# Two transformer blocks on one core: stationary and streamed tiles at other distances modulo 512 bytes

## The chip, the cores and the metric

The kernel runs on one core of a Trainium2 chip. The metric is the device time of one execution in microseconds, the median of several runs. Engines are named as in the profile: PE is TensorE's matmul, PEld its weight load, DVE is VectorE, ACT is ScalarE, POOL is GpSimd, and SPq is the DMA queue of SyncE.

## The reference

The input is one sequence of 256 rows of 2048 float32 values. Two unlike transformer blocks follow each other, and everything is float32. Cut to its matrix products, which are all that bears on the change:

```python
h = rms_norm(x, norm_mix_w);  proj = h @ w_in            # 2048 x 6160
x = x + concat(band_attention, gated_linear_attention) @ w_out      # 2048 x 2048
h = rms_norm(x, norm_ffn_w);  u = conv(h @ w_ffn_up)     # 2048 x 11264
x = x + (gelu(u_gate) * u_val) @ w_ffn_down              # 5632 x 2048
x = x + sigmoid(rms_norm(x) @ w_ple_gate) * (p @ w_ple_proj)
h = rmsnorm(rms_norm(x)); proj = h @ w_in_2              # 2048 x 8704
x = x + (sigmoid(ga) * (ya @ w_branch_a) + sigmoid(gb) * (yb @ w_branch_b)) @ w_out_2
x = x + swiglu(rmsnorm(x), w_ffn_in_2, w_ffn_down_2);  out = rmsnorm(x)
```

## The kernel before, in words

**Three matmuls for one product.** A float32 operand is split into a high part, rounded to the type F32R, and a low part, the rest. A product is then hi x hi + hi x lo + lo x hi, each with operands of type F32R. The activations are split once per stage into a pair of stationary tiles. The names of these pairs are AH/AL, BH/BL, XH/XL, ZH/ZL, MH/ML and the small PTH/PTL. The weights are split chunk by chunk as they arrive.

**The stream.** A chunk is two k-tiles of 128 rows by 512 columns, 512 KB. SP loads it into one of four slots of WR (L332), ACT copies WR to WH (L900), DVE subtracts to get WL (L1253), and PE runs `chunk` (L456 to L466): for both k-tiles and both row blocks of 128 it multiplies three times, 12 matmuls per chunk. There are 892 chunks (C_END, L71). Each matmul loads a block of 128 x 128 float32 of the stationary tile (512 bytes of each partition) and streams 512 columns of WH or WL (2048 bytes of each partition) past it into a bank of `acc`. So every matmul has a weight load of its own. In `chunk`:

```python
pe.matmul(o, H[:, kt + k, cols], WH[:, s, k], start=begin, stop=False)
pe.matmul(o, H[:, kt + k, cols], WL[:, s, k], start=False, stop=False)
mm = pe.matmul(o, L[:, kt + k, cols], WH[:, s, k], start=False, stop=end)
```

**The order of the work.** Every engine has a program written out by hand, and semaphores tie them. PE waits for `lo_done` of each chunk and for `acc_free` of each output tile. SP waits for `hi_done` and `lo_done` four chunks back, ACT for `chunk_used`. Between chunks PE runs transposes that the next stage needs (`turn` L488, `turn_four` L591, `turn_u` L712, `turn_h` L862). The stages are: in1, softmax and gated linear attention, out1, up1, down1, proj and ple, in2, the two attentions, branches, out2, up2, down2.

**Memory.** `sb` (L134) hands out SBUF: without `at` it takes the next free byte, rounded to 64; with `at` a tile lies where it is told, over others whose time is another. From `place` come vec, ss, ssum, a pad to 2048, X, `stationary`, AH, AL, WR, WH, WL, junk, six masks of 512 bytes, and three tiles of 64 bytes. `base` is the next multiple of 512, and everything of one stage alone lies from `base` on. With the sizes of the tiles this puts each of the tiles in question at 0 modulo 512: AH and AL, the four slots of WR, WH and WL, BH, BL, XH, XL, ZH, ZL, MH, ML, PTH and PTL. Each block of a stationary tile begins at a multiple of 512 too (256 columns of 4 bytes for a k-tile, 128 for a row block).

**The one exception.** The gate logits (L614 to L616) are 48 F32R matmuls whose stationary tiles WGH and WGL begin at 0 modulo 512, but are read from column 16 k on for k = 0 to 15, that is at 64 k bytes. They stream 256 columns of AH or AL, which begin at multiples of 1024:

```python
cols = slice(k * RANK, k * RANK + P)
pe.matmul(tp[:, 0, 0:T], WGH[:, cols], AH[:, k], start=(k == 0), stop=False)
```

Of the kernel before, what the change touches and what calls it, by code (L numbers as in the profile page):

```python
# [12 lines left out]
F32R = mybir.dt.float32r  # L13
# [4 lines left out]
P = 128  # L18
T = 256
TB = T // P  # L20
D = 2048
KT = D // P
# [7 lines left out]
HEADS = 16  # L30
# [18 lines left out]
FKT = FF // P  # L49
# [74 lines left out]
def two_blocks_kernel(nc, x, p, norm_mix_w, w_in, rel_bias, w_gate_up, b_gate, gla_norm_w, w_out, norm_ffn_w,  # L124
# [3 lines left out]
    with ctx:  # L128
# [3 lines left out]
        place = [nc.sbuf_base + (-nc.sbuf_base) % 64]  # L132

        def sb(name, shape, dt=F32, at=None):  # L134

            size = 4
            for n in shape[1:]:
                size *= n
            size += -size % 64
            if at is None:  # L140
                at = place[0]
                place[0] += size
            else:
                ends.append(at + size)
            return nc.alloc_sbuf_tensor_at(name, shape, dt, offset=at)
# [10 lines left out]
        stationary = place[0]  # L156
        AH = sb("AH", [P, KT, T], F32R)
        AL = sb("AL", [P, KT, T], F32R)
        WR = sb("WR", [P, RING, CHUNK_KT, NT])
        WH = sb("WH", [P, RING, CHUNK_KT, NT], F32R)  # L160
        WL = sb("WL", [P, RING, CHUNK_KT, NT], F32R)
# [7 lines left out]
        smean = sb("smean", [P, TB])  # L169
        sroot = sb("sroot", [P, TB])  # L170
        inv = sb("inv", [P, 7, TB])
        base = place[0] + (-place[0]) % 512
        assert stationary % 2048 == 0 and base % 512 == 0

        P1 = sb("P1", [P, TB, GATE1], at=base)
        o1 = base + TB * GATE1 * 4
# [35 lines left out]
        ZL = sb("ZL", [P, KT, T], F32R, at=o1 + 16384)  # L212

        BH = sb("BH", [P, FKT, T], F32R, at=base)
        BL = sb("BL", [P, FKT, T], F32R, at=base + FKT * T * 4)
        o3 = base + 2 * FKT * T * 4
        U = sb("U", [P, 2, TB, NT], at=o3)
        CV = sb("CV", [P, 2, 4, T], at=o3 + 8192)
        SG = sb("SG", [P, TB, NT], at=o3)
# [15 lines left out]
        o4 = base + TB * GATES2 * 4 + TB * 2 * D * 4  # L235
# [8 lines left out]
        rsum2 = sb("rsum2", [P, HEADS, 2], at=o4 + 25728)  # L244
        rrec2 = sb("rrec2", [P, HEADS, 2], at=o4 + 25856)
        rmax2 = sb("rmax2", [P, HEADS, 2], at=o4 + 25984)
        sk = sb("sk", [P, HEADS], at=o4 + 32768)
        sk2 = sb("sk2", [P, HEADS, 2], at=o4 + 32832)
        dist = sb("dist", [P, 2 * P], at=o4 + 32960)
        QKB = sb("QKB", [P, PAIRS, 2, T], at=stationary + 16384)  # L250
        SM = sb("SM", [P, 4, SCORES_FREE], at=o4)
        SE = sb("SE", [P, 4, SCORES_FREE], at=o4 + 6144)
        SA = sb("SA", [P, 2, SCORES_FREE], at=o4 + 12288)
        XH = sb("XH", [P, KT, T], F32R, at=o4)
        XL = sb("XL", [P, KT, T], F32R, at=o4 + 16384)
        MH = sb("MH", [P, KT, T], F32R, at=base)
        ML = sb("ML", [P, KT, T], F32R, at=base + 16384)
        assert max(ends) <= nc.sbuf_usable_end, (max(ends), nc.sbuf_usable_end)
# [40 lines left out]
        def slices_scaled(first):  # L299

            return lambda n: (x_scaled, first + n + 1)
# [11 lines left out]
        def rows(w, kt, cols):  # L313

            return w[kt * P:(kt + CHUNK_KT) * P, cols].rearrange("(a p) n -> p a n", p=P)
# [6 lines left out]
        def _(sp):  # L322
            def load(w, kt, cols, base, j, it=None, per=0):
# [4 lines left out]
                if not first:  # L328

                    sp.wait_ge(hi_done, at - RING + 1)  # L330
                    sp.wait_ge(lo_done, at - RING + 1)
                sp.dma_start(WR[:, n % RING], rows(w, kt, cols)).then_inc(w_loaded[n % RING], 16)  # L332

# [119 lines left out]
        def _(pe):  # L453
# [14 lines left out]
            def tile(H, L, nk, base, j0, a, count, it=None, per=0, each=1, kt0=0, between=None, groups=None):  # L468

                pe.wait_ge(acc_free[a], count if it is None else count + each * it)  # L470
                for q in range(nk // CHUNK_KT):
                    if groups is not None:
                        pe.wait_ge(turned_lo, groups + kt0 // 2 + q + 1)
                    chunk(H, L, kt0 + CHUNK_KT * q, base, j0 + q, a, q == 0, q == nk // CHUNK_KT - 1, it, per)
                    if between is not None:
                        between(q)
# [25 lines left out]
            def turned_tile(src, group, H, L, nk, base, a, count, ready=None, ahead=False, also=None):  # L502


                if not ahead:
                    turn(src, group, range(4), ready)

                def rest(q):
                    if also is not None:
                        also(q)  # L510
                    if q < 4 and nk == KT:
                        turn(src, group, [4 + q], ready)
                    elif q < 2:
                        turn(src, group, [4 + 2 * q, 5 + 2 * q], ready)

                tile(H, L, nk, base, 0, a, count, groups=group, between=rest)

            def loop_tiles(H, L, base, count, i0, i1, nk):

                with pe.Fori(i0, i1) as i:  # L520
                    tile(H, L, nk, base, 0, 0, pair(count, 0), i, nk)
                    tile(H, L, nk, base, nk // 2, 1, pair(count, 1), i, nk)
# [56 lines left out]

            turned_tile(x_cols, G_X1, AH, AL, KT, C_IN1, 0, A_IN1, lambda n: (x_in[n], 16), also=turn_convs)  # L580
            pe.wait_ge(masks, 6)
            tile(AH, AL, KT, C_IN1, 8, 1, A_IN1)
            loop_tiles(AH, AL, C_IN1, A_IN1, 1, GATE1 // NT // 2 - 1, KT)

# [21 lines left out]
            def gate_logits(q):  # L606
                if q == 0:
# [4 lines left out]
                    for k in range(KT):  # L612
                        cols = slice(k * RANK, k * RANK + P)
                        pe.matmul(tp[:, 0, 0:T], WGH[:, cols], AH[:, k], start=(k == 0), stop=False)  # L614
                        pe.matmul(tp[:, 0, 0:T], WGH[:, cols], AL[:, k], start=False, stop=False)
                        mm = pe.matmul(tp[:, 0, 0:T], WGL[:, cols], AH[:, k], start=False, stop=(k == KT - 1))  # L616
# [13 lines left out]
            n = GATE1 // NT // 2 - 1  # L630
            tile(AH, AL, KT, C_IN1 + 16 * n, 0, 0, A_IN1 + n, between=turn_band)
            tile(AH, AL, KT, C_IN1 + 16 * n, 8, 1, A_IN1 + n, between=gate_logits)

# [106 lines left out]
            for n in range(D // NT):  # L740
                tile(BH, BL, FKT, C_DOWN1, n * FKT // 2, n % 2, A_DOWN1 + n // 2,
                     between={0: last_u, D // NT - 1: turn_p}.get(n))
# [6 lines left out]

            turned_tile(x_cols, G_X2, XH, XL, KT, C_IN2, 0, A_IN2, slices_scaled(X_PLE), ahead=True)  # L750
            tile(XH, XL, KT, C_IN2, 8, 1, A_IN2)
            loop_tiles(XH, XL, C_IN2, A_IN2, 1, 7, KT)

# [22 lines left out]

            tile(XH, XL, KT, C_IN2, 112, 0, A_IN2 + 7)
            tile(XH, XL, KT, C_IN2, 120, 1, A_IN2 + 7, between=turn_stick)
            tile(XH, XL, KT, C_IN2, 128, 0, A_IN2 + 8, between=turn_window)

# [100 lines left out]
            pe.wait_ge(hb_lo, 2 * (FF // NT) - 2)  # L881
            tile(BH, BL, FKT, C_DOWN2, 0, 0, A_DOWN2[0], between=last_h)
            tile(BH, BL, FKT, C_DOWN2, FKT // 2, 1, A_DOWN2[1])
            loop_tiles(BH, BL, C_DOWN2, A_DOWN2, 1, 2, FKT)


        @block.scalar
        def _(act):
            def hi(base, js, it=None, per=0):

                for j in js:
# [6 lines left out]
                    if it is not None or n >= RING:  # L898
                        act.wait_ge(chunk_used, at - RING + 1)
                    act.activation(WH[:, n % RING], WR[:, n % RING], ACT.Copy).then_inc(hi_done, 1)  # L900

# [342 lines left out]
        def _(dve):  # L1244
            def lo(base, js, it=None, per=0):

                for j in js:
                    n = base + j
                    if n >= C_END:
                        continue  # L1250
                    at = n if it is None else n + per * it
                    dve.wait_ge(hi_done, at + 1)
                    dve.tensor_tensor(WL[:, n % RING], WR[:, n % RING], WH[:, n % RING].bitcast(F32),  # L1253
                                      ALU.subtract).then_inc(lo_done, 1)
# [241 lines left out]
            def up1(it, split):  # L1496
# [13 lines left out]
                dve.wait_ge(h_hi, it + 1)  # L1510
                dve.tensor_tensor(BL[:, bass.ds(it * 4, 4), :], CV[:, 0], BH[:, bass.ds(it * 4, 4), :].bitcast(F32),
                                  ALU.subtract).then_inc(h_lo, 1)
# [177 lines left out]
            def up2(it, split):  # L1690
# [8 lines left out]
                for b in range(2):  # L1699
                    dve.wait_ge(hb_hi, 2 * it + b + 1)  # L1700
                    cols = bass.ds(it * 4 + 2 * b, 2)
                    dve.tensor_tensor(BL[:, cols, :].rearrange("p a t -> p (a t)"), tp[:, b, :],
                                      BH[:, cols, :].bitcast(F32).rearrange("p a t -> p (a t)"),
# [58 lines left out]
```

## Time and profile before

| what | value |
|---|---|
| median of 3 runs | 2778.41 us (2776.94 to 2784.59) |
| the profiled execution, its own time | 2780.06 us |
| its span, first to last instruction | 2778.3 us |
| mean granted TensorE clock | 0.969 |
| PE busy | 2718.0 us (98%), 12225 matmuls |
| PEld busy | 2237.2 us (81%) |
| DVE, ACT, POOL busy | 1462.7, 1333.2, 18.3 us |
| HBM read | 476.06 MB |
| DMA queue q1, share of 16 engines | 55.9% |

The profiled execution took 1.7 us more than its span, and its time is 1.65 us over the median. Busy time of PE counts overlapping matmuls once: a matmul's own duration is from its start to its modelled end, and the next one starts before that. How fast the stream goes is read from the distance of two starts.

### The profile page before, as it was taken

How to read it: one execution, taken by the hardware profiler on the slowest of the kernel's cores; microseconds unless marked ns; L12 is line 12 of the kernel's file. 1: busy time of each engine (PE TensorE's matmuls, PEld its weight loads, DVE VectorE, ACT ScalarE, POOL GpSimd, SP SyncE). 2: the span in 40 equal slices, each digit the busy share in tenths (PEclk: the TensorE clock that was granted, in tenths of full speed). 3: DMA queues.
4: the chain of work that ended last, by engine and by line, in shares of the span. 5: the costliest groups of instructions: out<-in, count | busy, mean ns of one | idle time of the engine just before them, and what ended most of it. 6: DMA issues, size and time to landing. Idle time of an engine off the chain costs nothing.

```text
span 2778.3 us, 35705 instructions
## 1 busy us (share of the span) xinstructions
PE 2718.0 (98%) x12225; PEld 2237.2 (81%) x12225; DVE 1462.7 (53%) x1670; ACT 1333.2 (48%) x1675; POOL 18.3 (1%) x40
## 2 busy tenths in 40 slices
PE   8999989999999999999999999999999999999998
PEld 6888668888888888888788887778888888888886
DVE  5554445666665654455655445346554545454443
ACT  5333434665656643346533444464465454444443
POOL 1000000000000000000000000000000000000000
PEclk9999679999999999999999999599999999999999
DMA  8665106666656666665566665015566666666554
GB/s 267 194 192 166 54 25 189 177 187 181 189 175 195 183 195 193 194 199 187 162 197 195 191 195 152 1 39 190 187 183 188 191 187 188 191 187 205 193 193 145
DMA packets 246519, 479.40 MB, mean 173 GB/s; under 512 B 14709, under 2 KB 14821, under 8 KB 246177
## 3 DMA queue, kind: packets, MB, share of 16 engines
q1 hardware_dynamic: 244992, 471.97, 55.9%
q0 software_dynamic: 1440, 6.25, 0.7%
q8 instruction: 58, 0.95, 0.1%
q14 instruction: 29, 0.23, 0.0%
HBM read 476.06 MB, written 2.10 MB: 172 GB/s over the span
## 4 chain that ended last, share of the span: by engine, by line
PE 96%; DVE 2%; ACT 1%; issue 1%; DMA 0%; SPq 0%; ACTq 0%; DVEq 0%
PE acc L463 29%; PE acc L465 29%; PE acc L464 29%; PE acc L552 2%; PE tp L488 1%; PE tp L536 1%; PE tp L712 1%; PE tp L535 1%; PE tp L543 1%; PE tp L792 0%; DVE WL L1253 0%; PE tp L810 0%; ACT WH L900 0%; PE tp L862 0%; PE tp L591 0%
## 5 line engine op out<-in xcount | busy, mean ns | idle before, releaser
L1253 DVE TENSOR_TENSOR WL<-WR,WH 128x1024 fp32r<-128x1024 f32 x892 | 1090.2, 1225 | 1120.7 <-ACT WH L900 1120.1
L900 ACT ACTIVATE WH<-WR 128x1024 fp32r<-128x1024 f32 x892 | 943.7, 1060 | 1240.2 <-PE acc L465 1229.7
L463 PE MATMUL acc<-WH,AH 128*128 128x512 f32 x2048 | 804.7, 393 | 0.0
L465 PE MATMUL acc<-WH,AL 128*128 128x512 f32 x2048 | 798.7, 390 | 0.0
L464 PE MATMUL acc<-WL,AH 128*128 128x512 f32 x2048 | 798.0, 390 | 0.0
L465 PEld LDWEIGHTS acc<-WH,AL 128*128 128x128 f32 x2048 | 385.0, 188 | 80.9
L463 PEld LDWEIGHTS acc<-WH,AH 128*128 128x128 f32 x2048 | 385.5, 188 | 78.9 <-issue 1.1
L464 PEld LDWEIGHTS acc<-WL,AH 128*128 128x128 f32 x2048 | 385.5, 188 | 78.1
L463 PE MATMUL acc<-WH,BH 128*128 128x512 f32 x704 | 274.6, 390 | 0.0
L465 PE MATMUL acc<-WH,BL 128*128 128x512 f32 x704 | 274.0, 389 | 0.0
L464 PE MATMUL acc<-WL,BH 128*128 128x512 f32 x704 | 273.9, 389 | 0.0
L463 PE MATMUL acc<-WH,XH 128*128 128x512 f32 x544 | 214.4, 394 | 3.4 <-DVE WL L1253 3.4
L465 PE MATMUL acc<-WH,XL 128*128 128x512 f32 x544 | 212.7, 391 | 0.0
L464 PE MATMUL acc<-WL,XH 128*128 128x512 f32 x544 | 212.3, 390 | 0.0
L465 PEld LDWEIGHTS acc<-WH,BL 128*128 128x128 f32 x704 | 132.2, 188 | 27.6
L463 PEld LDWEIGHTS acc<-WH,BH 128*128 128x128 f32 x704 | 132.2, 188 | 27.3
L464 PEld LDWEIGHTS acc<-WL,BH 128*128 128x128 f32 x704 | 132.2, 188 | 27.1
L463 PEld LDWEIGHTS acc<-WH,XH 128*128 128x128 f32 x544 | 102.6, 189 | 25.3 <-DVE WL L1253 4.3
L465 PEld LDWEIGHTS acc<-WH,XL 128*128 128x128 f32 x544 | 102.4, 188 | 21.9
L464 PEld LDWEIGHTS acc<-WL,XH 128*128 128x128 f32 x544 | 102.6, 189 | 20.7
L1491 DVE SCALAR_TENSOR_TENSOR CV<-tp,vec,CV 128x254 f32<-128x254 f32 (+1 forms) x176 | 76.5, 476 | 6.4
L463 PE MATMUL acc<-WH,ZH 128*128 128x512 f32 x128 | 51.7, 404 | 6.0 <-DVE P L1464 6.0
(266 smaller groups left out, 1790.5 us busy)
## 6 DMA issues: line engine op xcount, KB each, us to landing
WR<-in_w_in_dram SPq DMA_DIRECT2D x232, 512.0 KB, 4.3
WR<-in_w_ffn_up_dram SPq DMA_DIRECT2D x176, 512.0 KB, 3.8
WR<-in_w_ffn_down_dram SPq DMA_DIRECT2D x176, 512.0 KB, 4.7
WR<-in_w_ffn_in_dram SPq DMA_DIRECT2D x176, 512.0 KB, 3.6
WR<-in_w_out_dram SPq DMA_DIRECT2D x64, 512.0 KB, 3.9
WR<-in_w_ple_gate_dram SPq DMA_DIRECT2D x32, 512.0 KB, 4.1
WR<-in_w_branch_a_dram SPq DMA_DIRECT2D x16, 512.0 KB, 3.8
WR<-in_w_branch_b_dram SPq DMA_DIRECT2D x16, 512.0 KB, 4.2
```

Of the source, the lines that this page charges most:

```text
L463: pe.matmul(o, H[:, kt + k, cols], WH[:, s, k], start=begin, stop=False)
L464: pe.matmul(o, H[:, kt + k, cols], WL[:, s, k], start=False, stop=False)
L465: mm = pe.matmul(o, L[:, kt + k, cols], WH[:, s, k], start=False, stop=end)
L488: mm = pe.transpose(tp[:, n % 4, k * T + tb * P:k * T + (tb + 1) * P], src(2 * g + k, tb), ident[:])
L535: pe.matmul(o[:, 0:P], q_of(h, 0, P), k_of(h, 0, P), start=True, stop=True)
L536: pe.matmul(o[:, P:3 * P], q_of(h, P, T), k_of(h, 0, T), start=True, stop=True).then_inc(s_full, 1)
L543: mm = pe.transpose(tp[:, 2 + n % 2, b * P:(b + 1) * P], B[:, n % 2, b * P:(b + 1) * P], ident[:])
L552: mm = pe.matmul(o, B[:, n % 2, blk * P:(blk + 1) * P], v_of(h, kb), start=(kb == 0), stop=(kb == qb))
L712: mm = pe.transpose(tp[:, 2 * a + fb // 2, (fb % 2) * T + tb * P:(fb % 2) * T + (tb + 1) * P], U[:, a, tb, fb * P:(fb + 1) * P], ident[:])
L900: act.activation(WH[:, n % RING], WR[:, n % RING], ACT.Copy).then_inc(hi_done, 1)
L1253: dve.tensor_tensor(WL[:, n % RING], WR[:, n % RING], WH[:, n % RING].bitcast(F32), ALU.subtract).then_inc(lo_done, 1)
L1491: last = dve.scalar_tensor_tensor(CV[:, a, fb, back:T], tp[:, 2 * a + b, k * T:(k + 1) * T - back], cw[:, tap, bass.ds(f, 1)], CV[:, a, fb ...
```

## The change

The tiles from WR on move up by 256 bytes: WR, WH and WL now begin at 256 modulo 512, while AH, AL and X stay. `base` is rounded to 64 only and lands at 448 modulo 512, 64 bytes lower than before. BL gets 128 bytes of its own in front (64 modulo 512), and what lies at `o3` behind it moves along. XL gets 704 (128 modulo 512), and sk, sk2 and dist go up by 1024 to stay clear of it. No instruction, semaphore or wait is added, removed or reordered. Distances of the stationary tile ahead of the streamed one, modulo 512: all 0 before; after it 256 for AH and AL, 192 for BH, XH, ZH, ZL, MH and ML, 320 for BL and PTH and PTL, 384 for XL. For the gate logits, where AH and AL are the streamed side, it is 64 k before and 448 + 64 k after.

```diff
--- before.py
+++ after.py
@@ -156,6 +156,7 @@
         stationary = place[0]
         AH = sb("AH", [P, KT, T], F32R)
         AL = sb("AL", [P, KT, T], F32R)
+        place[0] += 256
         WR = sb("WR", [P, RING, CHUNK_KT, NT])
         WH = sb("WH", [P, RING, CHUNK_KT, NT], F32R)
         WL = sb("WL", [P, RING, CHUNK_KT, NT], F32R)
@@ -169,8 +170,7 @@
         smean = sb("smean", [P, TB])
         sroot = sb("sroot", [P, TB])
         inv = sb("inv", [P, 7, TB])
-        base = place[0] + (-place[0]) % 512
-        assert stationary % 2048 == 0 and base % 512 == 0
+        base = place[0] + (-place[0]) % 64
 
         P1 = sb("P1", [P, TB, GATE1], at=base)
         o1 = base + TB * GATE1 * 4
@@ -212,8 +212,8 @@
         ZL = sb("ZL", [P, KT, T], F32R, at=o1 + 16384)
 
         BH = sb("BH", [P, FKT, T], F32R, at=base)
-        BL = sb("BL", [P, FKT, T], F32R, at=base + FKT * T * 4)
-        o3 = base + 2 * FKT * T * 4
+        BL = sb("BL", [P, FKT, T], F32R, at=base + FKT * T * 4 + 128)
+        o3 = base + 2 * FKT * T * 4 + 128
         U = sb("U", [P, 2, TB, NT], at=o3)
         CV = sb("CV", [P, 2, 4, T], at=o3 + 8192)
         SG = sb("SG", [P, TB, NT], at=o3)
@@ -244,15 +244,15 @@
         rsum2 = sb("rsum2", [P, HEADS, 2], at=o4 + 25728)
         rrec2 = sb("rrec2", [P, HEADS, 2], at=o4 + 25856)
         rmax2 = sb("rmax2", [P, HEADS, 2], at=o4 + 25984)
-        sk = sb("sk", [P, HEADS], at=o4 + 32768)
-        sk2 = sb("sk2", [P, HEADS, 2], at=o4 + 32832)
-        dist = sb("dist", [P, 2 * P], at=o4 + 32960)
+        sk = sb("sk", [P, HEADS], at=o4 + 33792)
+        sk2 = sb("sk2", [P, HEADS, 2], at=o4 + 33856)
+        dist = sb("dist", [P, 2 * P], at=o4 + 33984)
         QKB = sb("QKB", [P, PAIRS, 2, T], at=stationary + 16384)
         SM = sb("SM", [P, 4, SCORES_FREE], at=o4)
         SE = sb("SE", [P, 4, SCORES_FREE], at=o4 + 6144)
         SA = sb("SA", [P, 2, SCORES_FREE], at=o4 + 12288)
         XH = sb("XH", [P, KT, T], F32R, at=o4)
-        XL = sb("XL", [P, KT, T], F32R, at=o4 + 16384)
+        XL = sb("XL", [P, KT, T], F32R, at=o4 + 16384 + 704)
         MH = sb("MH", [P, KT, T], F32R, at=base)
         ML = sb("ML", [P, KT, T], F32R, at=base + 16384)
         assert max(ends) <= nc.sbuf_usable_end, (max(ends), nc.sbuf_usable_end)
```

## Rows read from the trace of the kernel before

**Rows 1.** The page: engines (busy us, share of the span, instructions) and granted clock by slice.

```profile
PE 2718.0 (98%) x12225; PEld 2237.2 (81%) x12225; DVE 1462.7 (53%) x1670; ACT 1333.2 (48%) x1675; POOL 18.3 (1%) x40
PEclk9999679999999999999999999599999999999999
```

**Rows 2.** The page: the chain that ended last, by engine and by line.

```profile
PE 96%; DVE 2%; ACT 1%; issue 1%; DMA 0%; SPq 0%; ACTq 0%; DVEq 0%
PE acc L463 29%; PE acc L465 29%; PE acc L464 29%; PE acc L552 2%; PE tp L488 1%; PE tp L536 1%; PE tp L712 1%; PE tp L535 1%; PE tp L543 1%; PE tp L792 0%; DVE WL L1253 0%; PE tp L810 0%; ACT WH L900 0%; PE tp L862 0%; PE tp L591 0%
```

**Rows 3.** Groups by form: busy us, mean ns of one, idle us before it.

```profile
L463 PE MATMUL acc<-WH,AH 128*128 128x512 f32 x2048 | 804.7, 393 | 0.0
L463 PE MATMUL acc<-WH,BH 128*128 128x512 f32 x704 | 274.6, 390 | 0.0
L463 PE MATMUL acc<-WH,XH 128*128 128x512 f32 x544 | 214.4, 394 | 3.4 <-DVE WL L1253 3.4
```

**Rows 4.** Timeline of PE, a stretch of in2 without transposes: start us, us, instruction.

```profile
1559.70 0.39 PE L463 MATMUL acc<-WH,XH 128*128 128x512 f32 x1
1559.93 0.39 PE L464 MATMUL acc<-WL,XH 128*128 128x512 f32 x1
...
1599.82 0.39 PE L463 MATMUL acc<-WH,XH 128*128 128x512 f32 x1
```

**Rows 5.** Timeline of PEld, same stretch.

```profile
1559.93 0.19 PEld L465 LDWEIGHTS acc<-WH,XL 128*128 128x128 f32 x1
...
1561.29 0.19 PEld L465 LDWEIGHTS acc<-WH,XL 128*128 128x128 f32 x1
```

**Rows 6.** Timeline of PE at half the granted clock.

```profile
...
1380.83 0.63 PE L463 MATMUL acc<-WH,XH 128*128 128x512 f32 x1
...
1382.96 0.63 PE L465 MATMUL acc<-WH,XL 128*128 128x512 f32 x1
```

**Rows 7.** Timeline of PE in in1, two stretches that follow groups of transposes.

```profile
...
246.66 0.40 PE L464 MATMUL acc<-WL,AH 128*128 128x512 f32 x1
...
247.36 0.39 PE L464 MATMUL acc<-WL,AH 128*128 128x512 f32 x1
...
248.97 0.39 PE L465 MATMUL acc<-WH,AL 128*128 128x512 f32 x1
...
256.28 0.39 PE L464 MATMUL acc<-WL,AH 128*128 128x512 f32 x1
...
258.57 0.39 PE L465 MATMUL acc<-WH,AL 128*128 128x512 f32 x1
```

**Rows 8.** Timeline of PE in the gate logits, from the third of 48 matmuls.

```profile
...
265.67 0.28 PE L616 MATMUL tp<-AH,WGL 128*128 128x256 f32 x1
265.79 0.28 PE L614 MATMUL tp<-AH,WGH 128*128 128x256 f32 x1
...
266.14 0.28 PE L614 MATMUL tp<-AH,WGH 128*128 128x256 f32 x1
...
266.84 0.28 PE L614 MATMUL tp<-AH,WGH 128*128 128x256 f32 x1
...
267.20 0.28 PE L614 MATMUL tp<-AH,WGH 128*128 128x256 f32 x1
...
270.99 0.28 PE L616 MATMUL tp<-AH,WGL 128*128 128x256 f32 x1
```

**Rows 9.** Groups by form: transposes between the streams.

```profile
L488 PE MATMUL tp<-ident,X 128*128 128x128 f32 x160 | 25.5, 287 | 6.1 <-DMA X<-in_x_dram 6.1
L712 PE MATMUL tp<-ident,U 128*128 128x128 f32 x176 | 22.8, 272 | 0.0
L862 PE MATMUL tp<-ident,HB 128*128 128x128 f32 x88 | 11.4, 272 | 0.0
```

**Rows 10.** Groups by form: the two engines that split a weight chunk.

```profile
L1253 DVE TENSOR_TENSOR WL<-WR,WH 128x1024 fp32r<-128x1024 f32 x892 | 1090.2, 1225 | 1120.7 <-ACT WH L900 1120.1
L900 ACT ACTIVATE WH<-WR 128x1024 fp32r<-128x1024 f32 x892 | 943.7, 1060 | 1240.2 <-PE acc L465 1229.7 <-DMA WR<-in_w_in_dram 9.8
```

## The prediction

> **What bounds the kernel now.** I read the page's engine lines first: PE is busy for 98% of the span with 12225 matmuls, and the granted clock is 9 tenths or more in nearly every slice [rows 1]. The chain of waits says that this is not only overlap: 96% of the chain that ended last is PE, and three lines, L463 to L465, hold 29% each [rows 2]. So the end is set by the rate at which the stream of the 892 chunks [rows 10] goes through PE: 892 x 12 = 10,704 matmuls of 512 columns, of which [rows 3] show the L463 third for the three largest tiles, with no idle time before them worth naming.
>
> The mean of one (390 to 404 ns) is no price, since it reaches into the next matmul. The rate is the distance of two starts. In a stretch of in2 without transposes, the first start is at 1559.70 and the last at 1599.82 us with 178 matmuls, so 177 distances: 40.12 / 177 = **226.7 ns** [rows 4]. At 2.4 GHz, 512 columns at one per cycle are 213.3 ns. Each matmul is thus 13.3 ns, or 32 cycles, longer than its columns. At half the granted clock (1.2 GHz) the excess is gone: from 1380.83 to 1382.96 are five distances, 426 ns each, and 512 / 1.2 is 426.7 ns [rows 6]. The 32 cycles are therefore no fixed number of cycles per instruction. They appear when PE asks for its operands at the full rate. What runs beside each streaming is the next weight load, 0.19 us long, which starts at the same time as the matmul before its own [rows 4, 5]. My reading is that the two reads get in each other's way.
>
> All of the change hangs on this excess. Multiplied by 10,704 it is 143 us, 5% of the time, and every nanosecond per matmul is 10.7 us, or 0.4%.
>
> **The change part by part.** No instruction is added or taken away. The parts are the new distances of the stationary tiles from WH and WL (256 for AH and AL; 192 for BH, XH, ZH and MH; 320 for BL; 384 for XL), the same addresses as seen by ACT, DVE and DMA, and the small tiles at new places.
>
> ACT and DVE first. DVE takes 1225 ns for WL, and ACT 1060 ns for WH [rows 10]. Twelve matmuls take 12 x 226.7 = 2720 ns, so both together (2285 ns) are still inside one chunk, and ACT idles 1229.7 us for PE, DVE 1120.1 us for ACT [rows 10]. WR, WH and WL move together, so their distances from each other stay. I cost this at nothing; the cover is the 435 ns per chunk, so both would have to become a fifth slower before PE waits. The loads of WR still write whole runs of 2048 bytes; they land four chunks ahead and queue behind nothing new. Nothing. The new places of sk, sk2, dist, U, CV and the attention tiles are plain address shifts: nothing, with 3 us either way kept for the attention stages, where PE does wait for these engines (an estimate: 1.5% of the three slices of 69 us at a lower clock in [rows 1]).
>
> The stream. No row has its operands at the new distances, so its price has to be bounded by neighbours.
>
> The first neighbour: the same operands, out of step. After a group of transposes the distances are not 226.7 ns. From 246.66 to 248.97 are ten distances of 231.0 ns, with three of 233.3 ns at their head (to 247.36), and from 256.28 to 258.57 ten of 229.0 ns [rows 7]. Addresses are the same as in the settled stretch. So the settled excess, 32 cycles, is what a pattern reaches that repeats from matmul to matmul, after about ten of them; whenever it is upset, the two reads meet more often. Before the change every block, stationary or streamed, begins at 0 modulo 512, so each matmul finds its successor's load in the same relation, and the pattern can hold. After it, H and L blocks stand at unlike distances in the BH and XH streams (192 and 320; 192 and 384), and every third load breaks step; in the AH stream the distance is uniform but not zero, and for want of a row I price it the same. Price: the mean of the two stretches is 230.0 ns, +3.3 ns per matmul. I leave out those that are out of step already: [rows 9] hold 40, 22 and 11 groups of four or eight transposes, with others some 90, so about 1,000 of 10,704. 9,700 x 3.3 = **+32 us**. The far end is the head of the first stretch: 9,700 x 6.6 = +64 us.
>
> The second neighbour: other distances, other shape. The gate logits read their stationary tile at 64 k bytes, so the distance runs through all multiples of 64 modulo 512. From 265.67 to 270.99 us are 45 distances: 118.2 ns each for 256 columns, or 106.7 ns at 2.4 GHz [rows 8]. The excess is 11.5 ns, 1.8 ns less than in the stream. Three in a row take 0.35 us in one place and 0.36 us in another [rows 8], so the excess lies between 10.0 and 13.3 ns. Price: 10,704 x -1.8 = -19 us, with the ends -36 and 0 us.
>
> Between the two I take the first, +32 us. It has the stream's own shape, with 512 columns behind a load. In the gate logits load and matmul are of nearly the same length, so what ends a matmul there is as well the load, and a shorter excess need not show less meeting. The second has the better claim as to distance, which is why its rival gets a fourth of the chance. **Sum:** 2780.1 + 32 = 2812 us for the profiled execution; the median lies 1.7 us below that execution, so 2810 us.
>
> **A rule against it.** PE waits for its own load here, as the 32 cycles that vanish at the half clock suggest [rows 4, 6]. The Trainium skill, page "TensorE: Matmul & The Clock Gate", section "Step-by-step: what each phase is for", says that the streamed operand and the weight load have an independent read port each, and "SBUF — State Buffer", section "SBUF: two separate sides", that TensorE's port never waits for another. By that rule no distance matters and the time would be 2778 us.
>
> **The rivals.**
> - *No change.* The excess may be a toll on every weight load, wherever it lies: in [rows 4] it stays the same over 177 distances, through all the blocks of XH and all four slots of WH, and only the disturbed stretches leave it. Against it: at equal addresses the toll is not constant [rows 7]. Time: 2778 us. The rule above ends here too.
> - *Faster, as in the gate logits.* Aligned blocks would be the bad case, since both reads enter the same stretch of 512 bytes together; any other distance parts them. For it: 118.2 ns [rows 8]. Against it: that shape may be bound by its load. It decides if the settled distance falls under 225.9 ns. Time: 2778 - 19 = 2759 us, at best 2742.
> - *The excess goes wholly*, if the distances keep the reads apart for good: 2778 - 143 = 2635 us. For it only the half clock's 426 ns [rows 6]; against it, no row at the full clock, at any distance, comes near it on average.
> - *Much slower:* the reads lock against each other so that every matmul costs more than 233.3 ns. Over 2842 us. No row shows such a state for long.
>
> **How the numbers follow.** Slower out of step: 0.44. Much slower: 0.04. No change: 0.21. Faster as in the gate logits: 0.24. Excess gone: 0.07. A measurement of this kernel can tell about 0.3%, 8 us or 0.8 ns per matmul. That gives 0.48 for slower, 0.21 for the same, 0.31 for faster. The time is that of the likeliest case, 2810 us, whose own range is 2790 to 2842 us. The range of 8 in 10 reaches down to the best end of the gate logits, 2742 us, and up to the far end of the first neighbour with the 3 us of the attention stages, 2845 us. It leaves out the two extreme cases and tails of the others, under 0.2 together.
>
> **What would show each step.** In the profile after: starts of the plain in2 stretch 229 to 233 ns apart, against 226.7; the BH and XH streams worse than AH, if unlike distances break the pattern; no change at the half clock (426 ns); DVE 1225 and ACT 1060 ns as before; PE's share of the chain unchanged at 96%. The first step is wrong if the settled distance is 226.7 ns or less. The reading of two reads that meet is wrong if all tiles keep 226.7 ns exactly. The step on ACT, DVE and DMA is wrong if the chain shows new shares of DVE, ACT or DMA.

## The result, and the profile after

| | before | after |
|---|---|---|
| median | 2777.86 us (4 runs, 2776.94 to 2784.59) | 2804.61 us (4 runs, 2803.12 to 2804.95) |
| the profiled execution, its own time | 2780.06 us | 2804.66 us |
| its span | 2778.3 us | 2803.0 us |
| mean granted clock | 0.969 | 0.967 |

The changed kernel is slower: ratio 1.009, 95% interval 1.0073 to 1.0107, or 26.7 us between the medians. The forecast was 2810 us. Every engine has the same instructions in the same order as before.

The page of the changed kernel, in its lines for engines, clock, chain, and the two splitting groups:

```profile
...
PE 2744.0 (98%) x12225; PEld 2242.1 (80%) x12225; DVE 1462.8 (52%) x1670; ACT 1332.5 (48%) x1675; POOL 18.3 (1%) x40
...
PEclk9999679999999999999999999599999999999999
...
PE 96%; DVE 2%; ACT 1%; issue 0%; DMA 0%; SPq 0%; ACTq 0%; DVEq 0%
...
L1253 DVE TENSOR_TENSOR WL<-WR,WH 128x1024 fp32r<-128x1024 f32 x892 | 1090.3, 1225 | 1140.9 <-ACT WH L900 1140.5
L900 ACT ACTIVATE WH<-WR 128x1024 fp32r<-128x1024 f32 x892 | 943.2, 1060 | 1261.5 <-PE acc L465 1251.2
```

PE gains 26 us of busy time and keeps its 96% of the chain; DVE's 1225 ns and ACT's 1060 ns are those of [rows 10]; their idle time grows by 20 and 21 us. So the time came into the stream, as [rows 1, 2] had led one to look for it there. Where in the stream, the timeline of PE tells. Four plain stretches of the changed kernel, first and last start of each (in1 with AH, down1 with BH, in2 with XH, out2 with MH); between them lie 177, 172, 174 and 154 distances:

```profile
...
99.73 0.39 PE L465 MATMUL acc<-WH,AL 128*128 128x512 f32 x1
...
139.85 0.39 PE L465 MATMUL acc<-WH,AL 128*128 128x512 f32 x1
...
1099.70 0.40 PE L465 MATMUL acc<-WH,BL 128*128 128x512 f32 x1
...
1139.83 0.40 PE L463 MATMUL acc<-WH,BH 128*128 128x512 f32 x1
...
1559.72 0.40 PE L465 MATMUL acc<-WH,XL 128*128 128x512 f32 x1
...
1599.94 0.40 PE L465 MATMUL acc<-WH,XL 128*128 128x512 f32 x1
...
1989.70 0.39 PE L465 MATMUL acc<-WH,ML 128*128 128x512 f32 x1
...
2024.95 0.39 PE L463 MATMUL acc<-WH,MH 128*128 128x512 f32 x1
```

- AH/AL, distance 256: 40.12 us / 177 = **226.7 ns**, what [rows 4] had. Nothing has changed here.
- BH/BL, 192 and 320: 40.13 / 172 = **233.3 ns**, 6.6 more.
- XH/XL, 192 and 384: 40.22 / 174 = **231.1 ns**, 4.5 more.
- MH/ML, 192 both: 35.25 / 154 = **228.9 ns**, 2.2 more.

At half the granted clock nothing is lost: six distances take 2.56 us, 427 ns each, as in [rows 6].

```profile
...
1387.21 0.63 PE L463 MATMUL acc<-WH,XH 128*128 128x512 f32 x1
...
1389.77 0.63 PE L463 MATMUL acc<-WH,XH 128*128 128x512 f32 x1
```

Could ACT, DVE or the DMA queues be what the tiles now collide with, since the stationary tiles have new distances from everything that these touch in WR, WH and WL too? The end of down2 answers this: the last chunks are loaded and split, and PE runs alone. One window of it, first before, then after (us, then busy us and instructions of PE, PEld, DVE, ACT, POOL, then granted clock, DMA share, GB/s), with the first and last start of 15 distances in each:

```profile
2760.00:2764.00 4.00, 4.00 (x19) 3.31 (x18) 0.00 (x0) 0.00 (x0) 0.00 (x0) 1.00 0.00 0
...
2760.03 0.39 PE L464 MATMUL acc<-WL,BH 128*128 128x512 f32 x1
...
2763.43 0.39 PE L464 MATMUL acc<-WL,BH 128*128 128x512 f32 x1
```

```profile
2784.00:2788.00 4.00, 4.00 (x19) 3.22 (x18) 0.00 (x0) 0.00 (x0) 0.00 (x0) 1.00 0.00 0
...
2784.24 0.40 PE L463 MATMUL acc<-WH,BH 128*128 128x512 f32 x1
...
2787.74 0.40 PE L463 MATMUL acc<-WH,BH 128*128 128x512 f32 x1
```

With ACT, DVE and DMA all at rest, the distances are 3.40 / 15 = 226.7 ns before and 3.50 / 15 = 233.3 ns after, as in the middle of down1. The 6.6 ns arise within PE's own work.

The sum, with 3 x 704 matmuls of BH/BL, 3 x 544 of XH/XL (the counts of [rows 3]) and 768 of MH/ML and ZH/ZL: 2112 x 6.6 + 1632 x 4.5 + 768 x 2.2 = 13.9 + 7.3 + 1.7 = 23 us. It is a little high, since it prices every matmul as settled. From the start of a stage's first WL to that of the next stage's, the changed kernel takes 6 us more in down1, 6 in in2, 7 in down2 and about 1 in out1 and out2 together, 20 to 21 us with the rest; 4 us more lie in the attention of the second block. The two profiled executions are 24.6 us apart, the medians 26.7; the profiled execution before was itself 2.2 us over its median. Down1 shows the share of one stage: first the kernel before, then the changed one, each with a window over down1 and one over the attention of the second block (us, then busy us and instructions of PE, PEld, DVE, ACT, POOL, then granted clock, DMA share, GB/s):

```profile
993.00:1234.00 241.00, 241.00 (x1079) 199.60 (x1078) 119.86 (x113) 100.00 (x104) 0.72 (x1) 1.00 0.60 192
1723.00:1852.00 129.00, 116.13 (x537) 92.67 (x537) 56.77 (x141) 68.09 (x149) 0.00 (x0) 0.71 0.03 9
```

```profile
994.00:1241.00 247.00, 247.00 (x1077) 199.65 (x1077) 120.14 (x113) 99.48 (x103) 0.72 (x1) 1.00 0.59 187
1736.00:1869.00 133.00, 120.56 (x536) 96.48 (x535) 56.58 (x141) 67.99 (x149) 0.00 (x0) 0.68 0.03 9
```

Down1 takes 6 us more for the same number of matmuls within two. The attention stretch takes 4 us more in this execution, at a granted clock of 0.68 in place of 0.71. It is not the layout of the shared region alone that does this: the second experiment has the same region, and its profile shows 129 us at 0.71 (the row below). Why this execution took longer there stays open.

```profile
1738.00:1867.00 129.00, 116.16 (x538) 92.73 (x537) 56.72 (x142) 67.71 (x149) 0.00 (x0) 0.71 0.03 9
```

### The profile page after: what moved, and what is told of

Same layout as the page of the kernel before. It is cut to its first block, busy times and chain, and to the rows that moved or that the text cites. A ratio compares the mean times of both kernels' runs of the same rounds, so it can differ in the third digit from the quotient of the medians.

```text
span 2803.0 us, 35705 instructions
## 1 busy us (share of the span) xinstructions
PE 2744.0 (98%) x12225; PEld 2242.1 (80%) x12225; DVE 1462.8 (52%) x1670; ACT 1332.5 (48%) x1675; POOL 18.3 (1%) x40
## 4 chain that ended last, share of the span: by engine, by line
PE 96%; DVE 2%; ACT 1%; issue 0%; DMA 0%; SPq 0%; ACTq 0%; DVEq 0%
PE acc L463 29%; PE acc L465 29%; PE acc L464 29%; PE acc L552 2%; PE tp L488 1%; PE tp L536 1%; PE tp L712 1%; PE tp L535 1%; PE tp L543 1%; PE tp L792 0%; DVE WL L1253 0%; PE tp L810 0%; PE tp L862 0%; PE tp L591 0%; DMA X<-in_x_dram 0%
## 5 line engine op out<-in xcount | busy, mean ns | idle before, releaser
L1253 DVE TENSOR_TENSOR WL<-WR,WH 128x1024 fp32r<-128x1024 f32 x892 | 1090.3, 1225 | 1140.9 <-ACT WH L900 1140.5
L900 ACT ACTIVATE WH<-WR 128x1024 fp32r<-128x1024 f32 x892 | 943.2, 1060 | 1261.5 <-PE acc L465 1251.2
```

## The experiments

Each is read by the mean distance of starts in a plain stretch at full clock, since a stage with few disturbances repeats it to 0.1 or 0.2 ns from run to run. "Distance" is that of the stationary block ahead of the streamed slot, modulo 512 bytes; an "even" distance is one that the high and the low tile share. The edits of 1, 3, 7, 8 and 9 are against the kernel before, those of 2, 4, 5, 6 and 10 against the changed kernel. Experiments 5 to 10 are one execution each, beside one of the kernel before: 2778.96 us for 5 to 7, 2779.64 us for 8 to 10.

**1. Everything moved by 64 bytes together (`e1_all_by_64`).**

```diff
+        place[0] += 64
         stationary = place[0]
...
-        base = place[0] + (-place[0]) % 512
-        assert stationary % 2048 == 0 and base % 512 == 0
+        base = place[0] + (64 - place[0]) % 512
```

> The kernel before with AH and everything behind it moved up by 64 bytes, so every stationary block and every streamed slot begins at 64 modulo 512 and all distances stay 0. If only the distance counts: 226.7 ns from start to start in the plain streams of AH, BH and XH, 2778 us. If it counts where a stationary block itself begins (one that does not begin at 0 modulo 512 reaches over a boundary): 230 to 235 ns in all streams, AH too, so 2778 + 9,300 x 3 to 8 ns = 2806 to 2852 us.

Measured: 2779.06 us, ratio 1.0005 (0.9995 to 1.0014). The BH stream, 177 distances:

```profile
...
1099.74 0.39 PE L464 MATMUL acc<-WL,BH 128*128 128x512 f32 x1
...
1139.86 0.39 PE L464 MATMUL acc<-WL,BH 128*128 128x512 f32 x1
```

That is 40.12 / 177 = 226.7 ns; AH and XH give the same 40.12 us for 177. No block of these streams begins at 0 modulo 512 any more, and it costs nothing. So where an operand lies by itself doesn't count, here at 64. That how the two lie to each other does count, experiment 5 shows: AH and AL at the same 64, with the stream at 0.

**2. The stream back at 0, the shared region left at 448 (`e2_region_only`).**

```diff
         AL = sb("AL", [P, KT, T], F32R)
-        place[0] += 256
...
-        base = place[0] + (-place[0]) % 64
+        base = place[0] + (448 - place[0]) % 512
```

> The changed kernel with WR, WH and WL back at 0 modulo 512; the shared region stays at 448, BL at 64, XL at 128. Distances: AH and AL 0, BH, XH, ZH, ZL, MH and ML 448, BL 64, XL 128. If only where the stationary block begins counts: the distances from start to start are those of the changed kernel, 233.2 ns for BH and BL, 231.3 for XH and XL, 2803 us. If the distance to the stream counts: AH at 226.7 ns, and the others move to values of their own, not those of the changed kernel; the time is then open between 2778 and 2815 us, and the two kernels differ by over 1 ns in at least one stream.

Measured: 2803.37 us, ratio 1.0092 (1.0076 to 1.0109). BH/BL at 448 and 64 run at 233.3 ns, MH/ML at 448 at 228.9 ns: the values of the changed kernel, which had 192/320 and 192. XH/XL at 448 and 128, with 172 distances, run at 40.27 / 172 = 234.1 ns, against 231.1 ns for 192 and 384:

```profile
...
1559.71 0.40 PE L463 MATMUL acc<-WL,XH 128*128 128x512 f32 x1
...
1599.98 0.40 PE L464 MATMUL acc<-WH,XL 128*128 128x512 f32 x1
```

By itself this run would be a poor witness for the distance, since two of the three streams don't move. One does, by 3 ns, with its block starts unchanged, so the stream's place matters too. Adding 256 to a distance leaves most values alone, but not all.

**3. Only the stream moved, by 256 (`e3_stream_only`).**

```diff
         AL = sb("AL", [P, KT, T], F32R)
+        place[0] += 256
         WR = sb("WR", [P, RING, CHUNK_KT, NT])
```

> The kernel before with WR, WH and WL moved up by 256 and nothing else; all stationary tiles stay at 0 modulo 512, all distances are 256. AH ran at 226.7 ns at this distance in the changed kernel, so if distance or the block's own start is what counts, every stream runs at 226.7 ns and the time is 2778 us. If the BH and XH streams are slower for some reason of their own once the stream is at 256: 229 to 235 ns in them, 2790 us or more.

Measured: 2778.31 us, ratio 1.0001 (0.9992 to 1.0011); AH, BH, XH and MH at 226.7 ns. The part of the change that comes first in its description, the 256 bytes, is free as long as the stationary tiles stay at 0; the cost comes with the shared region.

**4. High and low tile at the same distance (`e4_same_hl`).**

```diff
-        BL = sb("BL", [P, FKT, T], F32R, at=base + FKT * T * 4 + 128)
+        BL = sb("BL", [P, FKT, T], F32R, at=base + FKT * T * 4)
...
-        XL = sb("XL", [P, KT, T], F32R, at=o4 + 16384 + 704)
+        XL = sb("XL", [P, KT, T], F32R, at=o4 + 16384)
```

> The changed kernel with BL and XL back at the start of BH and XH modulo 512, so that high and low tile have the same distance of 192. MH and ML, at 192 both, ran at 228.9 ns in the mean. If the values of the distances add up without regard to the pair: BH/BL and XH/XL both at 228.9 ns, so 2803 - 2,022 x 4.3 ns - 1,388 x 2.4 ns = 2791 us. If unlike distances are what costs: 226.7 ns, 2780 us. If neither matters and the streams differ by stage: 233.2 and 231.3 ns as in the changed kernel, 2803 us.

Measured: 2789.65 us, ratio 1.0049 (1.0032 to 1.0066). BH/BL, 175 distances (XH/XL give the same 228.9 ns):

```profile
...
1099.76 0.39 PE L463 MATMUL acc<-WH,BH 128*128 128x512 f32 x1
...
1139.81 0.39 PE L464 MATMUL acc<-WL,BH 128*128 128x512 f32 x1
```

40.05 / 175 = 228.9 ns, the value that MH/ML have at 192. So the stage makes no difference: an even distance of 192 costs 2.2 ns in every stream. The changed kernel's own offsets for BL and XL cost the rest, 15 us of its 27 by the medians and 13 by the distances (2112 x 4.4 + 1632 x 2.2 ns); the four executions of this run spread from 2787.43 to 2796.94 us.

**5. Five even distances in one kernel (`e5_even_distances`).** The core of the edit (small tiles of the same regions move along to stay clear):

```diff
+        place[0] += 64
         AH = sb("AH", [P, KT, T], F32R)
...
-        place[0] += 256
+        place[0] += (0 - place[0]) % 512
...
+        BH = sb("BH", [P, FKT, T], F32R, at=base + 128)
         BL = sb("BL", [P, FKT, T], F32R, at=base + FKT * T * 4 + 128)
...
+        XH = sb("XH", [P, KT, T], F32R, at=o4 + 448)
+        XL = sb("XL", [P, KT, T], F32R, at=o4 + 16384 + 448)
...
```

> One look that reads five distances at once: the stream at 0 modulo 512, high and low tile always at the same distance, AH/AL at 64, BH/BL at 320, XH/XL at 128, ZH/ZL at 384, MH/ML at 32 (small tiles moved only to make room). If the cost repeats every 256 bytes: 64 and 320 give one value, 128 and 384 another, and at least one of them is over 226.7 ns, since 192 and 448 gave 228.9. If any even distance off a multiple of 256 costs the same: 228.9 ns in all five. If the period is 512: 64 and 320 differ by over 0.5 ns, or 128 and 384 do.

Measured: 2849.39 us. AH/AL at 64 (172 distances) and XH/XL at 128 (173):

```profile
...
99.75 0.39 PE L468 MATMUL acc<-WH,AL 128*128 128x512 f32 x1
...
139.88 0.39 PE L466 MATMUL acc<-WH,AH 128*128 128x512 f32 x1
...
1599.65 0.39 PE L466 MATMUL acc<-WH,XH 128*128 128x512 f32 x1
...
1639.84 0.40 PE L468 MATMUL acc<-WH,XL 128*128 128x512 f32 x1
```

64 gives 40.13 / 172 = 233.3 ns, 128 gives 40.19 / 173 = 232.3 ns. The others: 320 and 32 at 233.3, 384 at 233.4 ns. So 64 and 320 agree, 128 and 384 don't (by about 1 ns): 256 is a near symmetry and not the period. Multiples of 512 make no difference: the blocks of a stationary tile and the slots of the stream lie that far apart, and a plain stretch keeps one pattern through all of them. And 192 with its 2.2 ns is mild; most distances cost 6.6 ns.

**6. Pairs with unlike distances (`e6_pairs`).** The edit is of the same kind: AL moved 256 behind AH, BH/BL at 384/448, XH/XL at 0/128, ZH/ZL at 0/192, MH/ML at 0/320.

> One look at pairs with unlike distances: the stream at 0 modulo 512, AH/AL at 0/256, BH/BL at 384/448, XH/XL at 0/128, ZH/ZL at 0/192, MH/ML at 0/320. If each distance has its price and the pair does not matter (a third of the loads is of L): AH/AL stays at 226.7 ns, ZH/ZL lies between 226.7 and 228.9 ns, at 227.4. If a change of distance within the pair costs in itself: ZH/ZL, XH/XL and MH/ML are over 229 ns though H is at 0, and AH/AL shows whether a step of 256 costs too (over 227.5 ns) or not.

Measured: 2799.02 us. AH/AL at 0/256 (178 distances) and XH/XL at 0/128 (173):

```profile
...
99.63 0.39 PE L467 MATMUL acc<-WL,AH 128*128 128x512 f32 x1
...
139.98 0.39 PE L468 MATMUL acc<-WH,AL 128*128 128x512 f32 x1
...
1559.80 0.40 PE L467 MATMUL acc<-WL,XH 128*128 128x512 f32 x1
...
1599.79 0.39 PE L466 MATMUL acc<-WH,XH 128*128 128x512 f32 x1
```

0/256 is 40.35 / 178 = 226.7 ns: still free. 0/128 is 39.99 / 173 = 231.2 ns, and 0/320 and 0/192 gave 231.1 and 231.0 ns. With a third of the loads at 192, whose even price is 2.2 ns, the price by parts for 0/192 would be 0.7 ns; measured are 4.3 to 4.4. The same sum by parts gives 0/128 1.9 ns and 0/320 2.2 ns, where 4.5 and 4.4 are measured. A step between two tiles of a pair costs in itself, unless it is 256. BH/BL at 384/448 are at 233.3 ns, the value of an even 384.

**7. One load in three with half the columns (`e7_half_load`).**

```diff
                         pe.matmul(o, H[:, kt + k, cols], WH[:, s, k], start=begin, stop=False)
-                        pe.matmul(o, H[:, kt + k, cols], WL[:, s, k], start=False, stop=False)
-                        mm = pe.matmul(o, L[:, kt + k, cols], WH[:, s, k], start=False, stop=end)
+                        half_ = slice(tb * P, tb * P + 64)
+                        pe.matmul(acc[0:64, a, tb, :], L[:, kt + k, half_], WH[:, s, k], start=False, stop=False)
+                        mm = pe.matmul(o, H[:, kt + k, cols], WL[:, s, k], start=False, stop=end)
```

> Leaves out work: L x WH is computed for the first 64 of each 128 rows only, so its weight load reads 64 columns in place of 128, and it runs second of the three; columns streamed stay 512. If the 32 cycles are a toll that each weight load takes from the stream that it runs beside: the stream during which the short load runs loses 16 cycles in place of 32, so the mean of the three distances falls by 2.2 ns, from 226.7 to 224.4 ns, and the time by 20 to 24 us. If the 32 cycles are a fixed cost of a matmul at full clock, whatever is loaded: 226.7 ns and 2778 us.

Measured: 2813.66 us, 35 us *more* for less to load. In in2, 175 distances:

```profile
...
1559.62 0.39 PE L466 MATMUL acc<-WL,XH 128*128 128x512 f32 x1
...
1599.83 0.39 PE L464 MATMUL acc<-WH,XH 128*128 128x512 f32 x1
```

40.21 / 175 = 229.8 ns. Both expectations fall. The run reads fewer bytes at the same distances of 0 and loses 3.1 ns per matmul. Half the columns aren't half the load's time either: its PEld rows show 0.13 us in place of 0.19. The run also swaps the last two products, so it isn't a pure test of length, and the next one was made for that.

**8. All loads with half the columns (`e8_all_half_loads`).** The core:

```diff
+                        o = acc[0:64, a, tb, :]
+                        cols = slice(tb * P, tb * P + 64)
                         pe.matmul(o, H[:, kt + k, cols], WH[:, s, k], start=begin, stop=False)
...
+            dve.memset(acc[:], 0.0).then_inc(zeroed, 1)
```

> Leaves out work: all three matmuls compute the first 64 of each 128 rows only (the rest of acc is set to zero once at the start), so every weight load reads 64 columns, all alike and at distance 0; 512 columns are streamed as before. If the 32 cycles are the toll of one load of 128 columns, in a pattern that repeats: 16 cycles, 220.0 ns from start to start and 2778 - 65 = 2713 us. If they belong to the streaming of 512 columns at the full clock: 226.7 ns and 2778 us. If the pattern cannot settle with a load of half the length, as in the run with one short load in three (229.8 ns): 229 ns or more, 2800 us.

Measured: 2814.24 us. In in2, 175 distances (128*64 in a row is the size of the block loaded):

```profile
...
1559.71 0.40 PE L468 MATMUL acc<-WH,XL 128*64 128x512 f32 x1
...
1599.97 0.39 PE L466 MATMUL acc<-WH,XH 128*64 128x512 f32 x1
```

40.26 / 175 = 230.1 ns. With half the columns per load (0.13 us each), the same order as before and distances of 0 throughout, each matmul takes 3.4 ns longer. So distance 0 is not cheap in itself: in these runs it is cheap together with loads of 128 columns. The matmuls also write only 64 of the 128 partitions of `acc` here; what of the 3.4 ns is due to that, this run can't tell.

**9. Half the columns per load (`e9_half_streams`).**

```diff
+                        for c in range(2):
+                            n_ = slice(c * 256, (c + 1) * 256)
+                            oc = acc[:, a, tb, n_]
+                            pe.matmul(oc, H[:, kt + k, cols], WH[:, s, k, n_], start=begin and c == 0, stop=False, skip_group_check=True)
...
```

> The kernel before with every streamed slot cut into two runs of 256 columns, each with its own weight loads: 21,408 matmuls of 256 columns, distances all 0. If the excess goes with the load: 106.7 + 13.3 = 120.0 ns each, 2778 + 10,704 x 13.3 ns = 2920 us. If it goes with the columns streamed (one cycle in 17): 113.3 ns, unless the load of 0.11 us itself binds, 2778 us to 2800 us.

Measured: 2917.02 us. In in2, 168 distances:

```profile
...
1559.79 0.28 PE L468 MATMUL acc<-WH,XL 128*128 128x256 f32 x1
...
1579.95 0.28 PE L468 MATMUL acc<-WH,XL 128*128 128x256 f32 x1
```

20.16 / 168 = 120.0 ns. The first expectation is met to 0.1 ns: 106.7 for the columns and the same 13.3 on top, for half the columns. So the excess is no share of the columns streamed: each matmul with its load has it once. Every matmul of this run has one load, so the run can't tell a cost of the load from one of the matmul. Nor does it rule out, by itself, that a load of 128 columns takes 120 ns at the least. Against that stand the transposes of [rows 9], which load 128 x 128 float32 each. Eight of them in the kernel before:

```profile
612.24 1.03 PE L712 MATMUL tp<-ident,U 128*128 128x128 f32 x8
```

The last lasts 0.27 us, so the starts are 0.76 / 7 = 0.109 us apart: such a load need not take 120 ns, though what streams past it here is shorter and not of type F32R.

**10. Five more even distances (`e10_fine`).** The edit is that of experiment 5 with 32, 224, 96, 480 and 160.

> One look at five more even distances with the stream at 0: AH/AL at 32, BH/BL at 224, XH/XL at 96, ZH/ZL at 480, MH/ML at 160. If 226.7 ns is the least that any distance gives, none is under it; if 0 and 256 are only two good places among many, at least one is at 226.7 ns or under it, which would make a version that beats both kernels. 32 gave 233.3 ns in the MH stream and should do so in the AH stream, if the stage does not matter: 2778 + 5,273 x 6.7 ns = 2813 us from it alone.

Measured: 2843.62 us. 32, 224, 160 and 480 all at 233.3 to 233.4 ns, 96 at 234.2 ns. None is under 226.7.

What the runs say of a distance, in ns from start to start of 512 columns at full clock:

| distance of high/low tile | ns | seen in |
|---|---|---|
| 0, 256 (even), 0/256 | 226.7 | before, after, 1, 3, 6 |
| 192, 448 (even) | 228.9 | after, 2, 4 |
| 0/128, 0/192, 0/320 | 231.0 to 231.2 | 6 |
| 192/384 | 231.1 | after |
| 128 (even) | 232.3 to 232.4 | 5 |
| 32, 64, 160, 224, 320, 384, 480 (even), 192/320, 448/64, 384/448 | 233.3 to 233.4 | after, 2, 5, 6, 10 |
| 96 (even), 448/128 | 234.1 to 234.3 | 10, 2 |

No distance tried beats the kernel before.

## Why the prediction was right

It was right in sign, in place of the cost and nearly in the total. The total owes something to luck: one term was priced at what it doesn't cost, and another at half of what it does. The signs that it named came in: the plain in2 stretch at 231.1 ns (229 to 233 named), BH and XH worse than AH, 427 ns at the half clock, DVE, ACT and PE's 96% unchanged.

**What bounds the kernel.** Right: PE has the same 96% of the chain, and 20 to 21 of the 24.6 us between the profiles are in the distance of starts. That the excess of 13.3 ns belongs to the weight load was a reading of the rows and is shown only in part: experiment 9 has it once per matmul and load (13.3 ns on 256 columns as on 512), and experiments 7 and 8 show that the size of the load changes it; a fixed cost of the matmul within it isn't excluded. The changed kernel's 427 ns confirm that the half clock hides it. That the excess depends on how the two operands lie to each other is shown by experiments 1 and 5: all moved by 64, 226.7 ns; only the distance at 64, 233.3 ns. The end of down2 shows that it takes no other engine.

**ACT, DVE, DMA, small tiles at nothing.** Right as far as can be told: the groups keep their means, the chain its shares. 3 us were kept for the attention stages; one profile shows 4 us there, at a lower granted clock, which experiment 2 doesn't show.

**The stream at +3.3 ns for 9,700 matmuls.** The sum, 32 us, came near the 26.7 us between the medians (20 to 21 us in the stream by the profiles); its parts did not. The step failed for AH and AL: "the distance is uniform but not zero, and for want of a row I price it the same". They are 6,144 of the 10,704 matmuls and cost nothing, since 256 is as good as 0. BH/BL cost 6.6 ns, twice the price and as much as the head of the disturbed stretch, taken for the far end [rows 7]; XH/XL 4.5, MH/ML and ZH/ZL 2.2. By the prediction's price AH and AL would have carried over half of the sum. Two errors of opposite sign met. That the total is near is luck to that extent, and no proof of the +3.3.

**The reason given, a pattern that repeats.** Half right. That unlike distances break something which even ones keep is shown by experiments 4 and 6: 0/192 costs 4.3 ns, where its parts would cost 0.7. But evenness does not save a stream either: with an even 320 every distance of starts in down1 is 233 or 234 ns, and with an even 64 they are 231 and 236 in turn in the stretch of in1 shown under experiment 5. Both are steady patterns and dear ones, with the same mean of 233.3 ns. The pattern settles; what it settles at depends on the distance.

**The rivals.** *No change* (0.21): refuted by the result, and as a toll that is the same wherever the load lies by experiments 1 and 5 together. The Trainium skill, page "TensorE: Matmul & The Clock Gate", section "Step-by-step: what each phase is for", gives the stream and the weight load independent read ports. The measurement decides against reading this as free of mutual delay: the same load and stream take 226.7 or 233.3 ns by their distance alone. *Faster, as in the gate logits* (0.24): wrong. The gate logits of the changed kernel, again 45 distances:

```profile
...
265.56 0.28 PE L616 MATMUL tp<-AH,WGL 128*128 128x256 f32 x1
...
270.89 0.28 PE L616 MATMUL tp<-AH,WGL 128*128 128x256 f32 x1
```

5.33 / 45 = 118.4 ns, against 118.2 in [rows 8]. Experiment 9 gives what that row lacked, an aligned stream of 256 columns: 120.0 ns. So at 256 columns the gate logits with their mixed distances are *cheaper* than an aligned stream, by 1.6 to 1.8 ns, and at 512 every distance tried but 256 is dearer than 0. That it is the distances which do this at 256 columns is likely but not shown, since the gate logits also read other tiles, in blocks that overlap from one k to the next. The neighbour with the right distance had the wrong shape, as the prediction feared. *The excess goes wholly* and *much slower* have no support: no settled stream of 512 columns with loads of 128 is under 226.7 or over 234.3 ns at the full clock.

## What to carry to other kernels

When matmuls with a weight load each follow one another without a gap, read the distance of starts against the columns at the granted clock, not the mean duration: all of this change sits in 2 to 7 ns there, and the busy shares don't show it. If such a stream is the bound, put stationary blocks and streamed runs at the same place modulo 256 bytes, high and low tiles alike, and test any other layout tile by tile, since one kernel can read a distance in each of its stages. The advice is measured for float32-sized operands (F32R), loads of 128 columns and streams of 512; with half the columns per load 0 was no longer at 226.7 ns, and at 256 columns per stream mixed distances were a little cheaper. When a sum meets the result, still compare it term by term.

## What the runs showed that I had not expected

- 256 bytes is a near symmetry (0 and 256, 192 and 448, 64 and 320, 224 and 480), but not a full one: 128 gives 232.3 and 384 gives 233.4 ns, and 192/384 gives 231.1 where 448/128 gives 234.1.
- Loads of half the columns make the stream slower: 230.1 against 226.7 ns, with all distances at 0. An explanation by a toll in proportion to the load's columns would want 220. What sets the 32 cycles of the settled aligned stream stays open, as does why 192 is milder than its neighbours 160 and 224 (233.3); no run here looks inside the two reads.
- The excess at 0 is 13.3 ns for 512 as for 256 columns, so in a kernel with shorter streams it is a larger share: 2917 us against 2780 for the same work.
